# A gated MLP's down products in layer 1: where ScalarE and VectorE make the activations' parts, relative to the weights' parts

## The reference, cut to what matters

```python
D_MODEL = 1024
SEQ = 256
DEPTH = 2
D_FF = 2816

def _conv_ffn(h, w_up, conv_w, conv_b, w_down):
    gate, val = jnp.split(h @ w_up, 2, axis=-1)
    return (jax.nn.gelu(_dwconv3(gate, conv_w, conv_b)) * val) @ w_down

f = _conv_ffn(_modulate(h, mod[3], mod[4]), ffn_w_up[layer], ffn_conv_w[layer], ffn_conv_b[layer], ffn_w_down[layer])
return _norm(DEEPNORM_ALPHA * h + mod[5] * f, ln_g[layer, 1], ln_b[layer, 1])
```

## Time and profile before

| | us |
|---|---|
| median of 3 runs | 1922.81 |
| lowest and highest run | 1922.34, 1926.96 |
| the profiled execution's own time | 1918.57 |
| the profiled execution's span | 1916.7 |
| PE busy, matmuls (share of the span) | 1659.6 (87%) |
| PE busy, weight loads | 1308.7 (68%) |
| DVE busy | 1094.3 (57%) |
| ACT busy | 633.0 (33%) |
| POOL busy | 83.9 (4%) |
| mean granted PE clock, share of full speed | 0.904 |

### The profile page before, as it was taken

How to read it: one execution, slowest core, us unless ns; L and a number is a source line. 1 busy time by engine, 2 the same in 40 slices (tenths; PEclk the granted TensorE clock), 3 DMA queues, 4 the chain that set the end, 5 groups by cost and what they waited for, 6 DMA issues and landing times. The chain is left out here.

```text
span 1916.7 us, 29370 instructions
## 1 busy us (share of the span) xinstructions
PE 1659.6 (87%) x12092; PEld 1308.7 (68%) x12092; DVE 1094.3 (57%) x1870; ACT 633.0 (33%) x1052; POOL 83.9 (4%) x112
## 2 busy tenths in 40 slices
PE   7999999588778799999999969899777678899966
PEld 5667777455578578888877756777544667678854
DVE  2384456975656465555442446546885645677734
ACT  4344323234121135222222244422443212366621
POOL 0000111100200000000000000000201010000000
PEclk8999999798789699999999979999886888889988
DMA  9311211373101124222231032212142010355520
GB/s 380 117 49 34 77 45 45 124 267 111 75 2 47 44 111 154 88 94 105 88 110 45 1 113 67 67 56 88 58 164 90 2 45 12 120 201 196 188 98 22
DMA packets 41476, 182.00 MB, mean 95 GB/s; under 512 B 4608, under 2 KB 5376, under 8 KB 33536
## 3 DMA queue, kind: packets, MB, share of 16 engines
q1 hardware_dynamic: 41344, 180.14, 26.4%
HBM read 179.07 MB, written 1.05 MB: 94 GB/s over the span
## 5 line engine op out<-in xcount | busy, mean ns | idle before, releaser
L234 PE MATMUL ps<-hr_in,wr_in 128*128 128x512 f32 (+1 forms) x544 | 220.5, 405 | 18.0 <-DVE wr_in L227 15.6
L236 PE MATMUL ps<-hr_in,wr_in 128*128 128x512 f32 (+1 forms) x544 | 208.4, 383 | 0.0
L235 PE MATMUL ps<-hr_in,wr_in 128*128 128x512 f32 (+1 forms) x544 | 208.4, 383 | 0.0
L234 PEld LDWEIGHTS ps<-hr_in,wr_in 128*128 128x128 f32 x544 | 107.8, 198 | 68.3 <-issue 33.7
L227 DVE TENSOR_TENSOR wr_in<-mix,wr_in 128x1024 fp32r<-128x1024 f32 x68 | 84.4, 1243 | 96.5 <-ACT wr_in L223 96.5
L234 PE MATMUL ps<-mix_r,work_r 128*128 128x512 f32 (+1 forms) x352 | 135.0, 383 | 1.5 <-DVE work_r L227 1.5
L235 PE MATMUL ps<-work_r 128*128 128x512 f32 (+1 forms) x356 | 134.7, 378 | 0.0
L227 DVE TENSOR_TENSOR work_r<-pr,work_r 128x2048 fp32r<-128x2048 f32 x38 | 87.0, 2289 | 73.3 <-ACT work_r L223 69.2
L236 PE MATMUL ps<-mix_r,work_r 128*128 128x512 f32 x320 | 125.1, 391 | 0.0
L2820 PE MATMUL ps<-mix_r,work_r 128*128 128x512 f32 x336 | 120.5, 400 | 2.3 <-DVE mix_r L227 2.3
L236 PEld LDWEIGHTS ps<-hr_in,wr_in 128*128 128x128 f32 x544 | 107.3, 197 | 19.7
(11 more groups left out here) (501 smaller groups left out, 3417.8 us busy)
## 6 DMA issues: line engine op xcount, KB each, us to landing
mix<-in_w_in SPq DMA_DIRECT2D x68, 512.0 KB, 3.5
pr<-in_w_up SPq DMA_DIRECT2D x28, 1024.0 KB, 4.9
pr<-in_ada_w SPq DMA_DIRECT2D x44, 512.0 KB, 6.4
ring<-in_w_up SPq DMA_DIRECT2D x16, 1024.0 KB, 4.9
ring<-in_ada_w SPq DMA_DIRECT2D x28, 512.0 KB, 4.5
pr<-in_w_down SPq DMA_DIRECT2D x14, 1024.0 KB, 4.9
pr<-in_ada_w SPq DMA_DIRECT2D x8, 1024.0 KB, 15.5
work<-in_w_out SPq DMA_DIRECT2D x16, 512.0 KB, 3.8
```

The source lines that it names most:

```text
L234: nc.tensor.matmul(out, sh, mh, start=first, stop=False)
L235: nc.tensor.matmul(out, sh, ml, start=False, stop=False)
L236: return nc.tensor.matmul(out, sl, mh, start=False, stop=last)
```

## The change

Both loops over `k` go through pairs. With three buffers (layer 1), the activations' parts of a pair are now made first, and the parts of one load of weights behind them: on DVE that of the same pair (`low(22 + p)` behind `x_low(2p)` and `x_low(2p + 1)`), on ACT that of the pair after (`high(23 + p)`). Before, DVE made `low(23 + p)` and ACT `high(24 + p)` ahead of the same two `x` parts. With two buffers (layer 0) the order stays as it was. PE, SP and POOL have the same instructions in the same order; no work is added or taken away.

```diff
@@ DVE
-            for k in range(KF):
+            for k in range(0, KF, 2):
                 n = KF + k // 2 + BUFFERS - 2
-                if k % 2 == 0 and k and n < LOADS:
+                if k and n < LOADS and BUFFERS == 2:
                     low(n)
-                if k >= AHEAD:
-                    x_low(k)
+                for i in range(max(k, AHEAD), k + 2):
+                    x_low(i)
+                if k >= AHEAD and BUFFERS == 3 and KF + 2 + (k - AHEAD) // 2 < LOADS:
+                    low(KF + 2 + (k - AHEAD) // 2)
+            for n in range(KF + 2 + (KF - AHEAD) // 2, LOADS if BUFFERS == 3 else 0):
+                low(n)
@@ ACT
-            for k in range(KF):
-                n = KF + k // 2 + 2 * (BUFFERS - 2)
-                if k % 2 == 0 and k and n < LOADS:
+            for k in range(0, KF, 2):
+                n = KF + k // 2
+                if k and n < LOADS and BUFFERS == 2:
                     high(n)
-                if k >= AHEAD:
-                    x_high(k)
+                for i in range(max(k, AHEAD), k + 2):
+                    x_high(i)
+                if k >= AHEAD and BUFFERS == 3 and KF + 3 + (k - AHEAD) // 2 < LOADS:
+                    high(KF + 3 + (k - AHEAD) // 2)
+            for n in range(KF + 3 + (KF - AHEAD) // 2, LOADS if BUFFERS == 3 else 0):
+                high(n)
```

## The result

| | before | changed |
|---|---|---|
| median, us (lowest to highest, runs) | 1924.88 (1922.34 to 1930.64, 4) | 1896.13 (1889.94 to 1902.35, 4) |
| ratio to before | | 0.9863, 95% interval 0.9841 to 0.9886 |
| the profiled execution's own time, us | 1918.57 | 1897.25 |
| its span, us | 1916.7 | 1895.4 |
| from the start of pair 1 to the start of the last matmul, us | 89.42 | 61.81 |

The kernel is faster by 1.4%, some 26 us. 1897.0 was forecast, in a range of 1891 to 1902. The two profiled spans differ by 21.3 us only, and the last two rows of the table say why: the stretch that the change touches became 27.6 us shorter, and it began 6.3 us later, behind work that is the same in both.

The account below looks back on a forecast made before the run. Layer 1's down products were taken as bound by a circle of waits among PE, ACT and DVE, not PE's work. Pairs -27.9, last blocks +2.1: -25.8 us; from the 1922.81 median, 1897.0 us was forecast, range 1891 to 1902.

Parts of the forecast that it names:

- The circle on ACT: Layer 1's down products: ACT's `high(24 + p)` waits for pair p - 1, holding `x_high` of pair p; PE idles 2.99 us.
- A pair costs 6.14 us: Layer 1's down products: without the long wait, pairs take 24 x 0.2333 + 0.54 us; six go from 62.17 to 36.84.
- The price of a stop: Between pairs: 0.54 us for PE's wait for its own last matmul and the slow first step, taken from layer 0.
- `low(24)` has 1.5 us to spare: Start of layer 1's pairs: DVE finishes `low(24)` by 1820.0, PE wants it for pair 2 at about 1821.5.
- The last blocks: End of layer 1's down products: PE waits 2.4 us for `low(32)`, then a clock slump; 18.56 becomes 20.6 us, +2.1.
- The slump of 1.52 us: Last blocks of layer 1: the clock falls behind PE's 2.4 us wait, as after 1.82 us in layer 0.
- lower bound of +0.5 (no slump): Last blocks of layer 1: their added cost if the clock does not fall behind the wait; upper bound +3.5.
- Everything else equal: Layer 0, PE, SP and POOL: order unchanged, cost 0; the 11.8 us behind the last matmul moves as one piece.
- Rival A: Pairs 1 to 7: short stops let the clock fall, each pair pays 1.52 us, 10.6 lost, 1907.6; chance 0.08.
- Rival B: Six pairs: PE waits for `low` of weights instead of `x_low`, 23.5 us back, 1920.5, no change; chance 0.04.
- Rival C: Pairs and last blocks: granted clock stays low through the whole stretch, +16.5 us, 1939.3, slower; chance 0.02.

## Why the prediction was right

*The circle on ACT.* Shown, and by taking it apart: with ACT's order alone the waits between pairs go, with DVE's alone they grow. The prediction spoke of both orders together; that DVE's alone would lose was worked out only afterwards.

*A pair costs 6.14 us.* Measured: 36.85 us for six, 36.84 forecast, and 28.00 from pair 1 to the last blocks where 27.88 was forecast. The price of a stop taken from layer 0 held in layer 1.

*`low(24)` has 1.5 us to spare.* It ended 1823.77 + 2.29 = 1826.1, and PE wanted it at 1827.75: 1.7 us. With ACT's order alone PE waited 0.52 us in this place, 0.2 us more than its stop, though not for `low(24)` but for the activations' part behind it.

*The last blocks.* Here is the one term that was mis-sized. The wait was 2.11 us of idle time; counted between the starts of matmuls, as the prediction counts, 2.28 us were lost where I had 2.4. The slump of 1.52 us behind it did not come in any of three traces of the changed kernel. The blocks took 18.95 us to their last start, not 20.6. The step that failed was to take the clock's fall behind 1.82 us in one trace of layer 0 for a rule: that same wait goes both ways. So the stretch gained 27.6 us and not 25.8. The term came to +0.4 us, just below its lower bound of +0.5 (no slump).

*Everything else equal.* The forecast for the profiled execution was a span of 1890.9, and it was 1895.4: 1.8 us better in the stretch, 6.3 worse ahead of it. The prediction set what lies ahead at 0, and 4.7 of the 6.3 us are the slump in layer 0's mixers told of above. The ratios, over several executions, give 26.3 us (0.9863), 26.3 and 28.2 (0.9853 of 1920.4), where the stretch gives 27.6. Whether the change has any part in that slump stays open; I know of no path from the edit to the work upstream.

*The number.* That the median of 1896.13 lies 0.9 us from 1897.0 is in part luck. The forecast was counted from a median before of 1922.81; with one more execution it is 1924.88, and single executions of the changed kernel lie from 1889.94 to 1902.35. What bears the prediction out is the stretch: 27.6 us gained, 25.8 forecast, and most of the difference is the slump that did not come.

*Rival A* (a slump at every pair) would have shown a clock below 1.00 from 1821 on; it was 1.00, and taking the stops away left it there. The Trainium skill ("TensorE: Matmul & The Clock Gate", the section on psum-queue depth-cycling) ties oscillation to frequent micro-idles; stops of 0.30 us every 6.1 us did not bring it here. *Rival B* appeared in the kernel with DVE's order alone. *Rival C* did not come: the windows of the result show 1.00.

## What to carry to other kernels

When an engine's list mixes large parts that wait for a buffer with small parts that wait for nothing, put the small ones first: the wait at the head of a list holds all that stands behind it, however short. Orders on two engines that feed each other are one edit; try each alone, and don't be surprised if one of them loses, as it did here. Removing a stop upstream of a late operand lengthens the wait for it, so cover that wait in the same step.

## What the runs showed of the hardware

The same wait, in the same place and with the same work around it, was followed by a fall of TensorE's clock in some executions and not in others. In the down products, by the length of PE's idle time: at 0.30 to 0.52 us never; at 1.8 us three of 8; at 2.1 to 2.3 us none of 4; at 2.56 us and at 2.96 us, one case each, it fell; at 2.99 us all 14; at 5.44 us all 7. Between pairs 7 or 8 steps of 0.43 us follow behind 2.99 us, and 12 behind 5.44 us. The fall need not come at once: behind 2.99 us up to four steps were still at the high level's 0.23 us. These are this kernel's places, and what precedes each differs, so the list is no threshold.

How long the low level lasts is not fixed either. Behind the 6.47 us of idle time in layer 0's mixers the granted clock was 0.50 over PE's next 2 us in all 11 traces, but the 95 matmuls there took 14.5 us in seven of them and 19.24 us in four.

Such differences are part of why executions of one kernel lie up to 15 us apart (1915.2 to 1930.6 for the kernel before, over all its runs), more than I had taken a measurement's uncertainty to be. How much each place adds to that spread was not measured.
